# The samples' state products placed between the matmuls of the gate projection's last two jobs

## The reference, cut to what matters

```python
# prompt: retention in chunks of 128 tokens
scores = einsum('bnihd,bnjhd->bnhij', qc, kc) * mask
o = einsum(scores, vc) + einsum(qc, R_prev) * dec_start      # R: state carried from chunk to chunk
# samples: one step of the recurrence, per sample b and head h
S = g * S + einsum('bhd,bhe->bhde', k_t, v_t)
o = einsum('bhd,bhde->bhe', q_t, S)                           # 4 heads x 8 samples of 128x128 times a vector
# both
o = o * rsqrt(mean(o * o) + EPS)
ret_out = o * silu(g)
mix = concat([ret_out, conv_out]) @ w_out
```

## Time and profile before

| | |
|---|---|
| time, median of 3 runs (lowest, highest) | 1209.98 us (1209.64, 1210.54) |
| time of the profiled execution | 1212.49 us |
| its span | 1210.7 us |
| TensorE busy | 1179.2 us, 97% |
| VectorE, ScalarE, GpSimd busy | 741.2, 409.4, 422.9 us |
| mean granted TensorE clock | 0.991 |

### The profile page before, as it was taken

The page is one execution under the profiler, slowest core; times in us unless marked ns, Lnnn a source line. Parts: engine busy times, 40 slices in busy tenths (PEclk is TensorE's granted clock), DMA queues, the critical chain, the costliest instruction groups (busy, mean ns, idle before and its releaser), DMA issues.

```text
span 1210.7 us, 21798 instructions
## 1 busy us (share of the span) xinstructions
PE 1179.2 (97%) x8411; PEld 1157.4 (96%) x8411; DVE 741.2 (61%) x1203; ACT 409.4 (34%) x718; POOL 422.9 (35%) x304
## 2 busy tenths in 40 slices
PE   7999999999999998799999999999999999999997
PEld 6999999999999986699999999999999999999997
DVE  5559899944455247965555555655656565656556
ACT  5444444333344245531313131313131313222223
POOL 3066788213122267431313132322222222222226
PEclk9999999999979999899999999999999999999999
DMA  9211111121144233121212020202011121212134
GB/s 311 87 35 53 35 53 53 36 72 36 36 139 114 88 122 116 44 71 36 71 35 69 17 87 0 88 16 86 18 59 45 40 64 35 69 35 69 36 143 173
DMA packets 99797, 84.49 MB, mean 70 GB/s; under 512 B 2722, under 2 KB 89378, under 8 KB 99738
## 3 DMA queue, kind: packets, MB, share of 16 engines
q1 hardware_dynamic: 99554, 83.61, 22.4%
q10 hardware_dynamic: 192, 0.17, 0.0%
HBM read 72.86 MB, written 11.38 MB: 70 GB/s over the span
## 4 chain that ended last, share of the span: by engine, by line
PE 91%; POOL 3%; DVE 3%; issue 2%; DMA 1%; ACT 1%; DVEq 0%; ACTq 0%; POOLq 0%
PE ps L356 28%; PE ps L358 28%; PE ps L357 28%; PE ps L1756 1%; POOL o_last L690 1%; POOL h_ring L663 1%; PE ps L1582 1%; PE ps L1621 1%; PE ps L1686 1%; PE ps L1705 1%; PE ps L1810 1%; PE ps L1809 1%; DMA t_sm<-table_identity_decays 1%; POOL st L546 1%; DVE w_ring L1409 1%
## 5 line engine op out<-in xcount | busy, mean ns | idle before, releaser
L356 PE MATMUL ps<-xn_hi,w_hi 128*128 128x350 f32 (+2 forms) x576 | 187.2, 325 | 0.3 <-DVE xn_lo L1114 0.2
L358 PE MATMUL ps<-xn_lo,w_hi 128*128 128x350 f32 (+2 forms) x576 | 185.2, 322 | 0.0
L357 PE MATMUL ps<-xn_hi,w_lo 128*128 128x350 f32 (+2 forms) x576 | 184.9, 321 | 0.0
L356 PE MATMUL ps<-x_hi,w_ring 128*128 128x256 f32 x616 | 174.2, 283 | 7.2 <-DVE w_ring L1409 6.3
L356 PE MATMUL ps<-x,w_ring 128*128 128x260 f32 x616 | 175.4, 285 | 1.6 <-issue 1.2
L357 PE MATMUL ps<-x,w_ring 128*128 128x260 f32 x616 | 175.3, 285 | 0.0
L358 PE MATMUL ps<-x,w_ring 128*128 128x260 f32 x616 | 175.0, 284 | 0.0
L358 PE MATMUL ps<-x_lo,w_ring 128*128 128x256 f32 x616 | 173.6, 282 | 0.0
L357 PE MATMUL ps<-x_hi,w_ring 128*128 128x256 f32 x616 | 173.5, 282 | 0.0
L356 PE MATMUL ps<-act_hi,fx_hi 128*128 128x388 f32 (+1 forms) x528 | 171.3, 324 | 0.3
L358 PE MATMUL ps<-act_lo,fx_hi 128*128 128x388 f32 (+1 forms) x528 | 168.5, 319 | 0.0
(11 more groups left out here) (232 smaller groups left out, 2496.4 us busy)
## 6 DMA issues: line engine op xcount, KB each, us to landing
f_raw<-in_w_ffn_in SPq DMA_DIRECT2D x42, 512.0 KB, 4.2
raw<-in_w_in SPq DMA_DIRECT2D x24, 512.0 KB, 3.9
f_raw<-in_w_ffn_out SPq DMA_DIRECT2D x22, 512.0 KB, 3.3
x_st<-in_x_prompt SPq DMA_DIRECT2D x8, 512.0 KB, 7.9
raw<-in_w_out SPq DMA_DIRECT2D x8, 512.0 KB, 5.6
h_ring<-in_x_prompt SPq DMA_DIRECT2D x8, 512.0 KB, 4.6
h_scratch<-h_ring SPq DMA_DIRECT2D x8, 512.0 KB, 3.0
h_fin<-h_scratch SPq DMA_DIRECT2D x8, 512.0 KB
```

Source lines behind the costliest of these rows:

```text
L356: nc.tensor.matmul(out, hi, mhi, start=first, stop=False, skip_group_check=resumes)
L357: nc.tensor.matmul(out, lo, mhi, start=False, stop=False, skip_group_check=resumes)
L358: return nc.tensor.matmul(out, hi, mlo, start=False, stop=last, skip_group_check=resumes)
```

## The change

Gate jobs 9, 10 and 11 move. Job 9 goes from the end of chunk 3 to the place ahead of the output of chunk 4. Jobs 10 and 11 go from chunk 4 to chunk 5, to where the samples' products stood. The samples' 32 products no longer stand in two blocks of 16: in each of jobs 10 and 11 one product of one column is issued behind the first matmul and one behind the second matmul of each step of k. `s_os` is raised by 2 at the end of each of the two jobs, and no longer by 1 per head. ScalarE's `g_silu(9)`, `g_silu(10)` and `g_silu(11)` move along. No instruction that computes is added or removed.

```diff
 ScalarE
                 if n < 5:
-                    g_silu(2 * n + 2)
+                    g_silu(2 * n + 2 if n < 3 else n + 5)
                 act.wait_ge(s_O, n + 1)
...
+                if n == 5:
+                    g_silu(10)
                 y_norm(n)
-                if n < 5:
+                if n < 3:
                     g_silu(2 * n + 3)
                 if n == 5:
+                    g_silu(11)
                     conv_hi(0)
                     ret_hi(0)
 TensorE
+            def sample_o(hh, b):
+                return mm(ps[:, 5, hh * NS + b:hh * NS + b + 1], state_sb[:, hh, b, :],
+                          qT[:, hh, META + SEQ + b:META + SEQ + b + 1], start=True, stop=True)
-            def g_job(j):
+            def g_job(j, heads=()):
...
+                if j == 10:
+                    pe.wait_ge(s_vbd, NS)
+                    pe.wait_ge(s_on, 4)
                 for k in range(KT):
-                    ins = three_pass(...)
+                    wh, wl = w_hi[:, r, k * P:(k + 1) * P], w_lo[:, r, k * P:(k + 1) * P]
+                    xh, xl = xn_hi[:, k, c0:c0 + n], xn_lo[:, k, c0:c0 + n]
+                    if not heads:
+                        ins = three_pass(ps[:, 6, 0:n], wh, wl, xh, xl, k == 0, k == KT - 1)
+                        continue
+                    nc.tensor.matmul(ps[:, 6, 0:n], wh, xh, start=k == 0, stop=False, skip_group_check=True)
+                    sample_o(heads[0], k)
+                    nc.tensor.matmul(ps[:, 6, 0:n], wl, xh, start=False, stop=False, skip_group_check=True)
+                    last = sample_o(heads[1], k)
+                    ins = nc.tensor.matmul(ps[:, 6, 0:n], wh, xl, start=False, stop=k == KT - 1, skip_group_check=True)
+                if heads:
+                    last.then_inc(s_os, 2)
                 ins.then_inc(s_job, 1)
...
-            def sample_o(hh):
-                if hh == 0:
-                    pe.wait_ge(s_vbd, NS)
-                    pe.wait_ge(s_on, 4)
-                for b in range(NS):
-                    ins = mm(...)
-                ins.then_inc(s_os, 1)
 chunk loop
                 if n < 5:
-                    g_job(2 * n + 2)
+                    g_job(2 * n + 2 if n < 3 else n + 5)
...
                 kv(kT[:, :, c], vT[:, :, c], P)
                 if n == 5:
-                    sample_o(0)
-                    sample_o(1)
+                    g_job(10, (0, 1))
                 if n >= 6:
                     out_job(2 * n - 12)
                 y_tok(n)
                 if n == 5:
-                    sample_o(2)
-                    sample_o(3)
-                if n < 5:
+                    g_job(11, (2, 3))
+                if n < 3:
                     g_job(2 * n + 3)
                 if n >= 1:
                     o_back(n - 1)
```

More of the change, by code:

```diff
@@ L1666, in g_job @@
                     pe.wait_ge(s_vg, CREDIT_AB + 12 + j)
+                if j == 10:
+                    pe.wait_ge(s_vbd, NS)
+                    pe.wait_ge(s_on, 4)
                 for k in range(KT):
-                    ins = three_pass(ps[:, 6, 0:n], w_hi[:, r, k * P:(k + 1) * P], w_lo[:, r, k * P:(k + 1) * P],
-                                     xn_hi[:, k, c0:c0 + n], xn_lo[:, k, c0:c0 + n], k == 0, k == KT - 1)
+                    wh, wl = w_hi[:, r, k * P:(k + 1) * P], w_lo[:, r, k * P:(k + 1) * P]
[10 more added lines that the diff above has]
+                    last.then_inc(s_os, 2)
                 ins.then_inc(s_job, 1)
@@ L1748, in y_back @@
                 ins.then_inc(s_ynT, 1)
-            def sample_o(hh):
-                if hh == 0:
-                    pe.wait_ge(s_vbd, NS)
-                    pe.wait_ge(s_on, 4)
-                for b in range(NS):
-                    ins = mm(ps[:, 5, hh * NS + b:hh * NS + b + 1], state_sb[:, hh, b, :],
-                             qT[:, hh, META + SEQ + b:META + SEQ + b + 1], start=True, stop=True)
-                ins.then_inc(s_os, 1)
             def out_job(i):
```

## The result

The changed kernel takes 1216.59 us in the median of 5 runs (1215.16 to 1218.83), the kernel before 1209.98 us (5 runs, 1209.53 to 1212.87). The ratio is 1.0054, 95% interval 1.0040 to 1.0067: slower by 6.6 us. Forecast was 1212.0 us with a range from 1207.4 to 1215.2.

The account below looks back on a forecast made before the run. TensorE's order was taken to bound the kernel, with the products and the half clock under them. A start of `out_job(0)` 0.8 us later plus 1.2 us of clock gave +2.0: 1209.98 becomes 1212.0 us, range 1207.4 to 1215.2.

Parts of the forecast that it names:

- (3): Job 10 with its 16 products: each costs two exposed weight loads, 0.214 us; 7.23 us in all.
- (7): Behind the new idle stretch of 3.8 us the clock may fall: 1.2 us lost, bounds 0 and 1.6.
- (1): Jobs 10 and 11 leave chunk 4, so the order ahead of the samples is 7.62 us earlier.
- (2): Chunks 3 and 4 lose cover; TensorE waits for `ret_out` 1.8 us, twice: +3.6 us.
- The bound of 0.107: Cost in us of a product in job 10 if the load of the long matmul cost nothing.
- rival B: Long matmuls' loads are cheap, a product costs 0.107 to 0.14 us: 1209.1 us, chance 0.2.
- (4): Job 11 waits for `g_silu(10)`, 0.55 us with hops, and runs 347.03 to 354.26; output weight loads cost nothing.
- (5): Full clock in jobs 10 and 11, half-clock stretches vanish; a gain of 3.0 us if nothing else were late.
- Rival C: Single columns bring the clock down in spite of the long matmuls: 1215.6 us, chance 0.1.
- (6): Hand-over behind job 11 takes 9.15 us, GpSimd holding up `ret_lo(0)`; `out_job(0)` starts 0.8 us later than before.
- Rival A: The chain behind job 11 is no longer than TensorE's own 5.3 us: -3.0, 1207.0 us, chance 0.1.

Follow-up runs that it names:

- experiment 1: The kernel before, unchanged, timed and profiled again, with three more profiles taken: ratio 1.0001.
- before_look_3: The kernel before, unchanged, one more profile to see half-clock stretch and time side by side: 1210.71 us.
- experiment 2: The changed kernel with the 16 products of each of jobs 10 and 11 in one block ahead of the job's matmuls: 1221.42 us.
- experiment 4: The changed kernel with weights split earlier, `ret_hi(0)` ahead of `conv_hi(0)`, and VectorE making the convolution half's low part: 1210.58 us.
- Experiment 3: The changed kernel with 34 transposes that nothing waits for, filling the idle stretch ahead of `out_job(0)`: 1214.34 us.

## Why the prediction was wrong, point by point

The places and the mechanisms were right, the size was not. Forecast +2.0 us, measured +6.6. Of the three outcomes that it gave chances, the one with 0.33, slower, came.

**The step that failed** is the last one of the sum, "The median of the runs, 1209.98, becomes 1212.0". It subtracts a cost read from one execution and adds the rest to the median of others, as if the 2.5 us between the two were the same in both kernels. For 1.6 of them they were a part of the cost that the change removes: in an execution near the median the half clock lasts 10.2 us and not 13.65, and that much less is there to be saved (experiment 1). The rows to distrust it by were at hand: 1212.49 us beside runs from 1209.64 to 1210.54. This step is the largest single part of the miss and not the whole. The terms (3) and (7) and one that the sum lacks were together some 1.5 us too small. The other 1.5 us lie outside the stretch that the change touches: 0.8 in the start of the one profiled execution, 0.7 between the typical execution used below (1210.71 us) and the median.

The term that the sum lacks: the first work behind a wait took longer than the same work in a running stream. By the chain, the transposes of k take 0.66 us behind each of the two waits where they took 0.44 in the kernel before, the first matmul of job 11 takes 0.42 us where job 10's takes 0.16, and the first of `out_job(0)` 0.44 where it took 0.18 before. This is 0.96 us in all.

**(1), (2)** Two waits of 1.79 us each, released by `ret_out`, as worked out (1.8). Job 10 starts 3.7 us before the place of the first product of before, when both are counted from the start of the chunk loop; 4.0 was worked out. The two longer groups of transposes, 0.22 us each, are about the difference.

**(3)** By the chain job 10 takes 7.39 us (340.31 to 347.70). A product costs 0.224 us between long matmuls ((7.39 - 3.81) / 16), 0.214 was taken: 0.16 us per job. The bound of 0.107 and rival B fall: behind a product the long matmul takes 0.26 us instead of 0.16, so the load of an fp32r matrix is not cheap where one column covers it. The Trainium skill, "TensorE: Matmul & The Clock Gate", section on weight-path perf modes, says that weights that aren't fp32 load faster; the prediction's estimate from it, 0.14 us a product, is not borne out for fp32r.

**(4)** Job 11 waited 0.54 us behind job 10, 0.55 was worked out, but took 7.65 us (348.24 to 355.89), with the 0.26 us of its first matmul. The output weights, issued from 347.49 on, held up nothing on TensorE.

**(5)** The full clock in jobs 10 and 11: right, and shown by experiment 2. Rival C falls.

**(6)** By the chain the hand-over took 9.12 us (355.89 to 365.01), 9.15 was worked out. Each of its steps is in the chain, with `ret_lo(0)` held up by GpSimd. Rival A falls. That the hand-over is what costs is shown by experiment 4.

**(7)** 1.6 us (120.4 us from `out_job(0)` to the feed-forward layer against 118.8), 1.2 was taken, and 1.6 was the upper bound. Experiment 3 shows that it is the idle stretch that causes it.

The bill by the profiles, from a typical execution of before (before_look_3, 97.6 us from the first transposes ahead of the chunk loop to `out_job(0)`) to the changed kernel (101.15 us): +3.6 us. From there to the feed-forward layer 118.8 against 120.4 us: +1.6, the clock. The start of the kernel was 0.8 us later in the changed kernel's profile (263.9 against 263.0), which is an execution's chance. The sum is 6.0 of the 5.9 us between these two executions. Of the first 5.1 us, 1.6 are the wrong base, 2.0 were forecast, and 1.5 are the terms above. The medians lie 6.6 us apart and not 5.9; the medians of the kernel before itself differ by up to 0.65 us between the groups of runs. The changed kernel's own five runs spread from 1215.16 to 1218.83 us and only one was profiled; why they spread stays open.

## What to carry to other kernels

When a slow piece of work is made faster or moved, ask what it covered: here two blocks of slow products hid a chain of nine microseconds over three engines, and taking 28 of their 32 products away was worth 1.6 us. Start the dependent chain from the last thing that it really needs, and shorten it, before the cover is removed; then work moved into the gaps pays (8 products in a gap of 1.8 us gave 1.4 us).

If the profiled execution is not at the median of the runs, find out which part of it differs before subtracting any of its parts. And where a new wait is added to a sum, add the slower first work behind it.

## What the hardware showed that was not expected

The same kernel's executions differ by 1.6 us through TensorE's clock alone: under the same blocks of single-column products it fell 2.4 to 2.8 us or 4.2 to 5.0 us after the first of them, and stayed at 0.50 for 13.65 or 10.24 us.

A product of a 128x128 fp32 state with one column costs 0.22 us whether it stands in a block at full clock or between matmuls of 348 columns (16 of them with a job take 7.39 us or 7.47 us from start to start, the job alone 3.90): a long matmul beside it hides nothing in sum.

Behind a wait of TensorE, the first matmul or group of transposes took 0.22 to 0.26 us longer than the same work in a running stream.
